# A two-part transformer kernel: constant-only products in TensorE's stream, taken out at the stage changes

## What is computed

```python
# block 1, layer 0: rwkv7 time mix; layer 1: latent attention (MLA)
x = x + rmsnorm(m, norm_g[layer, 1])
f = conv_ffn(rmsnorm(x, norm_g[layer, 2]), ...)      # D_FF = 2816, gelu(conv(gate)) * up
x = x + rmsnorm(f, norm_g[layer, 3])
# block 2, layer 0: differential attention; layer 1: indexed sparse attention (DSA)
x = x + mix
x = x + sq_relu_mlp(rms_norm(x, norm_mlp[i]), mlp_w1[i], mlp_w2[i])   # D_FF = 4096
```

## Time and profile before

| | us |
|---|---|
| median of 3 runs | 1431.79 (1431.6 to 1432.03) |
| the profiled execution, whole time | 1430.4 |
| its span, first to last instruction | 1428.4 |
| TensorE (PE) busy | 1386.9 (97%) |
| VectorE (DVE) busy | 944.3 (66%) |
| ScalarE (ACT) busy | 638.2 (45%) |
| mean granted TensorE clock | 0.996 of full |

### The profile page before, as it was taken

How to read it: one execution, slowest core, us unless ns; L and a number is a source line. 1 busy time by engine, 2 the same in 40 slices (tenths; PEclk the granted TensorE clock), 3 DMA queues, 4 the chain that set the end, 5 groups by cost and what they waited for, 6 DMA issues and landing times.

```text
span 1428.4 us, 22445 instructions
## 1 busy us (share of the span) xinstructions
PE 1386.9 (97%) x8874; PEld 1227.8 (86%) x8874; DVE 944.3 (66%) x1665; ACT 638.2 (45%) x949; POOL 52.1 (4%) x43
## 2 busy tenths in 40 slices
PE   8999999999999998999999999999999998999998
PEld 6885999789999887899999787889998787889997
DVE  6776467676777776577767587665555677565554
ACT  4431121453443657544333667544342568543341
POOL 1002000000000002000000100000000042000000
PEclk9999999999999999999999999999999999999999
DMA  7532001365553332365554351584631423464610
GB/s 247 190 107 97 33 2 60 117 208 187 195 177 126 129 134 80 118 224 189 176 177 146 118 177 60 208 310 175 227 126 59 156 67 111 173 242 174 230 64 30
DMA packets 110959, 208.15 MB, mean 146 GB/s; under 512 B 3840, under 2 KB 53248, under 8 KB 110368
## 3 DMA queue, kind: packets, MB, share of 16 engines
q1 hardware_dynamic: 110880, 207.06, 41.6%
HBM read 205.99 MB, written 1.05 MB: 145 GB/s over the span
## 4 chain that ended last, share of the span: by engine, by line
PE 86%; DVE 7%; ACT 5%; issue 1%; DMA 0%; DVEq 0%; SPq 0%; ACTq 0%
PE ps L931 20%; PE ps L827 12%; PE ps L912 10%; PE ps L917 10%; PE ps L909 10%; PE ps L1161 4%; PE ps L978 2%; PE ps L1281 2%; PE ps L1070 2%; PE ps L967 1%; PE ps L890 1%; PE ps L1324 1%; PE ps L1435 1%; PE ps L1338 1%; PE ps L1520 1%
## 5 line engine op out<-in xcount | busy, mean ns | idle before, releaser
L1672 ACT CAST Ah<-ringA 128x2048 fp32r<-128x2048 f32 x76 | 145.1, 1909 | 275.8 <-PE ps L917 258.8
L2321 DVE TENSOR_TENSOR Al<-ringA,Ah 128x2048 fp32r<-128x2048 f32 x76 | 174.1, 2291 | 98.7 <-ACT Ah L1672 98.4
L2328 DVE TENSOR_TENSOR Bl<-ringB,Bh 128x1024 fp32r<-128x1024 f32 (+1 forms) x76 | 127.0, 1670 | 52.5 <-ACT Bh L1681 52.5
L912 PE MATMUL ps<-hTl,Ah 128*128 128x256 f32 x1152 | 160.4, 281 | 0.0
L917 PE MATMUL ps<-hTh,Al 128*128 128x256 f32 x1152 | 159.9, 281 | 0.0
L909 PE MATMUL ps<-hTh,Ah 128*128 128x256 f32 x1152 | 159.7, 281 | 0.0
L1681 ACT CAST Bh<-ringB 128x1024 fp32r<-128x1024 f32 (+1 forms) x76 | 107.3, 1412 | 112.7 <-PE ps L931 112.4
L909 PEld LDWEIGHTS ps<-hTh,Ah 128*128 128x128 f32 x1152 | 151.0, 188 | 5.3
L912 PEld LDWEIGHTS ps<-hTl,Ah 128*128 128x128 f32 x1152 | 147.2, 189 | 0.0
L917 PEld LDWEIGHTS ps<-hTh,Al 128*128 128x128 f32 x1152 | 146.2, 189 | 0.0
L931 PE MATMUL ps<-Bh,hidh 128*128 128x512 f32 x432 | 135.0, 394 | 8.2 <-issue 6.6
(11 more groups left out here) (421 smaller groups left out, 2189.7 us busy)
## 6 DMA issues: line engine op xcount, KB each, us to landing
ringA<-in_ffn_w_in SPq DMA_DIRECT2D x44, 1024.0 KB, 7.3
ringA<-in_mlp_w SPq DMA_DIRECT2D x32, 1024.0 KB, 7.6
ringB<-in_mlp_w SPq DMA_DIRECT2D x32, 1024.0 KB, 6.8
ringB<-in_ffn_w_out SPq DMA_DIRECT2D x44, 512.0 KB, 4.1
ringA<-in_diff_w_in SPq DMA_DIRECT2D x12, 1024.0 KB, 6.2
ringA<-in_dsa_w_in SPq DMA_DIRECT2D x8, 1024.0 KB, 6.2
ringA<-in_w_k SPq DMA_DIRECT2D x4, 1024.0 KB, 8.4
ringA<-in_w_r SPq DMA_DIRECT2D x4, 1024.0 KB, 7.2
```

Of the source, the lines that this page charges most:

```text
L912: mm(o, Ah[:, half, k * T + j * P:k * T + j * P + P], hTl[:, k, :], start=False, stop=False)
L1672: nc.scalar.copy(a_split(w, Ah, half), a_half(w, ap, half)).then_inc(ah_rdy, 1)
L2321: V.tensor_tensor(a_split(w, Al, half), a_half(w, (a_at[w] + par) % 2, half), a_split(w, Ah, half).bitcast(F32), ALU.subtract).then_inc(al ...
L2328: V.tensor_tensor(Bl[:, half, 0:n], ringB[:, (G0[w] + par) % 2, half * n:(half + 1) * n], Bh[:, half, 0:n].bitcast(F32), ALU.subtract).the ...
```

## The change

All calls of `warm` and `keep` are taken out, and the two helpers with them. Nothing else is changed.

```diff
                             last = mm(dst, x[:, t, k * P:(k + 1) * P], diag[:, t, :],
                                       start=True, stop=True)
-                            if t == 0 and k == KT - 1:
-                                if name == "n0":
-                                    warm(6)
-                                else:
-                                    keep(2, 0)
...
-            def warm(n):
-
-                for _ in range(n):
-                    mm(ps[:, 7, 0:P], ident, ident, start=True, stop=True)
-
-            def keep(n, b):
-
-                for _ in range(n):
-                    mm(ps[:, b, 0:T], ident, con[:, 0:T], start=True, stop=True)
...
             pe.wait_ge(early_in, 16)
-            warm(6)
             turn16("n0")
             pe.wait_ge(con_in, 16)
-            keep(10, 7)
...
             turn16("o0")
-            keep(3, 3)
             out_proj(0)
-            keep(7, 7)
             turn16("nf0")
             ffn("ffn0", 1)
...
                 for h in range(heads):
-                    if diff and h == heads - 2:
-                        keep(3, 3)
                     turn(h)
...
-            keep(6, 7)
             turn16("n1")
...
             out_proj(1)
-            keep(7, 7)
             turn16("nf1")
             ffn("ffn1", 1)
-            keep(6, 7)
             turn16("n2")
...
-            keep(6, 3)
             turn16("o2")
...
             sin_jobs(4)
-            keep(7, job_bank(J["k3"][0]))
             pe.wait_ge(pre["src"], 3)
```

## The result

The changed kernel takes 1437.88 us in the median of 9 runs (1434.5 to 1440.48), the kernel before 1431.6 (1429.81 to 1433.63, 9 runs). The ratio is 1.0037, 95% interval 1.0026 to 1.0048: slower by 5.3 us (3.7 to 6.9). The profiled execution took 1437.97 us, 7.6 over the 1430.4 of the one before. The spread grew too: its nine times lie in two clusters, four at 1434.5 to 1435.4 and five at 1437.9 to 1440.5.

A forecast was written before the change was run, and what follows sets the result against it. TensorE, busy 97% of the span, was taken to bound the kernel. Six large gaps at 9.3, +0.5 at n0 and -0.9 at out_proj(0) gave +8.9 on 1431.8: 1440.7 us, range 1434.5 to 1449.

The forecast's parts named there:

- rival B: Falls come but are cheap, 3.4 us each, about 0.8 a place: +4.2, 1436 us; chance 0.17.
- The six gaps: Idle times left ahead of nf0, nf1, n1, n2, o2 and k3, 3.15 to 3.85 us; 11.2 us if all fall.
- Rival A: The clock holds in nearly all gaps, only queue effects are left: 1429.2 to 1430.9 us; chance 0.08.
- n0, +0.5 taken: First norm and lora products: sooner start against half-clock stretches, bounds -1.7 and +3.4, taken +0.5 us.
- out_proj(0), -0.9: o0 to out_proj(0): the next real product waits behind filler, so removal gains 0.9 us; bounds 0 and -1.3.
- nf0 and nf1, 1.0 each: Ahead of nf0 and nf1: 3.8 us idle, then half clock on t=0 and part of t=1; 1.0 us each.
- n1, 1.0: ffn0 to n1: 3.15 us idle, cold TensorE partly covered by ScalarE's evictions; 1.0 us, bounds 0 and 3.
- n2, o2 and k3, 3.0, 3.0 and 2.2: Gaps followed by transposes at n2, o2, k3: two half-clock lengths, less cover; 3.0, 3.0 and 2.2 us.
- inside attend(1), 0: Inside attend(1): 1.8 us idle, shorter than any that led to a fall; 0 us, bounds 0 and 3.
- A term that was put at nothing: +2.8 at mlp0: mlp0's 2.80 us wait from 932.75 passed without a fall and served as evidence; no cost was forecast there.
- the 1.9 taken off for a large gap that would hold: Six large gaps: one in six was let hold its clock, which lowered 11.2 to 9.3 us.
- Rival C: Falls last longer, through all transposes, and are more, including attend(1)'s short gap: 17.5 us slower, 1449; chance 0.10.

The follow-up runs named there:

- e8: e5 with keep(3, 3) ahead of out_proj(0) taken out: 1429.34 us, ratio 0.9979 to the kernel before.
- e4: Kernel before with each warm and keep product replaced by transposes of constants of about the same busy time: 1432.17 us, ratio 1.0003.
- e5: Kernel before with keep(5, 7) added in the 2.80 us waits of mlp0 and mlp1: 1428.86 us, ratio 0.9978.
- e3: Kernel before without the products ahead of n1, n2, k3 and o2 and inside attend(1): 1437.19 us, ratio 1.0045.
- e11: e5 without the products ahead of n1, n2, k3 and o2 and inside attend(1): 1432.64 us, ratio 1.0011 to the kernel before.
- e6: Changed kernel with keep(5, 7) in mlp0 and mlp1 and no other product of constants: 1433.27 us, ratio 1.0011 to the kernel before.
- e1: Kernel before without the products at n0 and keep(3, 3) ahead of out_proj(0): 1433.21 us, ratio 1.0014.
- e2: Kernel before without keep(7, 7) ahead of nf0 and nf1 and keep(2, 0) inside them: 1437.68 us, ratio 1.0029.
- e7: Kernel before with half of each keep, rounded up: 1434.28 us, ratio 1.0014.
- e9: e5 without the products at n0 and keep(3, 3) at out_proj(0): 1430.78 us, ratio 0.9994 to the kernel before.
- e12: Kernel before with keep(7, 3) in place of keep(3, 3) ahead of out_proj(0): 1434.23 us, ratio 1.0021.
- e10: e5 without keep(7, 7) ahead of nf0 and nf1 and keep(2, 0) inside: 1432.05 us, ratio 1.0006 to the kernel before.

## Why the prediction was right, and where its steps failed

The forecast was +8.9 us and 1440.7; measured are 5.3 by the ratio and 1437.88. Sign, mechanism and range hold. The size is less good than it looks: 5.3 lies nearer to rival B's 4.2 than to 8.9, and the range was wide enough to take in both. The six gaps have the forecast lengths, and the clock fell in all six of the profiled execution. Rival A (the clock holds) is out, by the windows of after. By its terms, held against the account above:

- *n0, +0.5 taken.* Measured -0.4 by 55.80 us, behind an idle time of 2.88 us and not of 4. The fall came, at 16.48, but the lora's first group took it up: it started 1.1 us sooner and the rest started at 19.98 against 19.90.
- *out_proj(0), -0.9.* Measured -0.8, and 0.8 again in e8. Right in size there; e8 shows that the median need not gain by it.
- *nf0 and nf1, 1.0 each.* Measured +0.7 and +0.9, for another reason than given: the half clock lasted 6.8 us and not 3.4, and the wait for the first hidden part gave 0.5 back.
- *n1, 1.0.* Measured 0.0. The transposes ended 0.8 us later (483.75 + 3.38 against 484.18 + 2.18), while ScalarE paced the evictions; the next products started at the same lead as before. The cover that the prediction called partial was whole.
- *n2, o2 and k3, 3.0, 3.0 and 2.2: the step that failed.* It said that behind a gap with transposes the clock stays at half for two lengths, from one case at 142 us. Measured +1.1, +1.5 and +1.5. At n1, n2 and k3 the stretch was 3.41 us, though transposes filled all or most of it; only o2, with more than 2 us of idle in its 6.8, had two. e4 shows that transposes are no lesser work for the clock. The case at 142 us was read for its kind of instruction; e5's window from 141.53, 3.4 us with transposes, shows that it also comes in one length. Nor is one length the rule: k3 had 10.24 us of half clock in e3 and e11, so the length is not settled by the kind of work that follows, and what settles it was not found.
- *inside attend(1), 0.* Measured +0.4: a gap of 1.78 us between other short waits did fall.
- *A term that was put at nothing: +2.8 at mlp0.* The prediction used the 2.80 us wait at 932.75 as evidence that such a gap may pass, and did not ask what it would cost if it fell in the changed kernel. e5 and e6 show it: with mlp0 and mlp1 filled, the kernel before gains 3.1 and the changed one 3.7 us.

By the account the places of the change make 7.6 - 2.8 + 0.1 = 4.9 us in that execution. That the total landed near the forecast is in part luck: one overestimate (8.2 forecast on n2, o2 and k3 against 4.1) stands against one omission (2.8), and n0 and n1, 1.9 too dear together, against the 1.9 taken off for a large gap that would hold, where all six fell.

Rival B had the better total and the better price a place, about 0.8, and half its reason: of the six large gaps n1, n2 and k3 had 3.4 us of half clock, nf0, nf1 and o2 had 6.8. Rival C's short gap and second length at nf0 and nf1 came true, its total not.

**What stays open.** The parts cost more than the whole, with mlp0 and mlp1 filled or not. The profiled executions of e1, e2, e3, e7, e8, e9, e11 and e12 show falls that before's doesn't have at places that the edit leaves alone (n1, attend(0) and mlp0, from 487 to 495, 538 to 550 and 935 to 946 us). Unfilled, mlp0 fell in after, e1, e2, e3, e7 and e12 and passed in before and e4.

Some of this is chance of the execution and not of the edit. Up to the stretch at 142 us the kernels of before, e2, e3, e5, e8, e10, e11 and e12 are the same, yet it has 6.8 us in before, e2, e8 and e10 and 3.4 us in the others, which is worth 1.2 to 1.4 us. The four that have 3.4 got there 0.2 to 0.6 us sooner than before, the other three later; but after, e1, e6 and e9, with other work at their start, came 0.2 to 0.4 sooner and had 6.8. That the moment at which a gap comes decides is in line with this, with e1, e2 and e12, but e12's interval doesn't exclude the plain shift, and why a partial removal should meet the bad moments more often than the full one was not found. Prices for single places from one trace are therefore good for that trace only.

## What to carry to other kernels

A TensorE that idles 2 to 4 us at a stage change can lose time behind the gap as well as in it (2.8 us behind mlp0's 2.80 in one execution, nothing in another): look at the granted clock and the duration of the first instructions behind each wait, and fill every such gap, not only those of which one trace shows that the clock fell. Filler is free where the timeline shows idle time behind its last product, and it delays what stands behind it where the next real instruction starts at once (0.8 us at out_proj(0), which the median did not show). Compare such variants by many runs and by their mean clocks, and don't add up parts that were measured alone.

## What was not expected of the hardware

- Equal waits fall or pass: e7's nf0 fell behind 2.06 us of idle and its nf1 passed with 2.05; mlp0's 2.80 us passed before and was followed by 6.8 us of half clock after. The kernel before itself ran from 1428.59 us at a mean clock of 0.998 to 1434.12 at 0.993, beside e5 to e8.
- The half-clock stretches between matmuls in all these traces were 3.4, 6.8 or 10.2 us long.
- 31.7 us of TensorE work of no use, in the right places, is worth 5.3 us of time, and 20 more such instructions in two places (10 products, some 4.6 us busy) another 3.1.
